# Dilated attention: the queries' and keys' transposes placed between the column blocks of their projection, and the first token tile's merge placed inside the item loop

## The chip, the cores and the metric

The kernel runs on one core of a Trainium2 chip. The metric is the device time of one execution in microseconds; the time before is the median of three executions. TensorE is written PE for its matmuls and PEld for its weight loads, VectorE is DVE, ScalarE is ACT, GpSimd is POOL and SyncE is SP.

## The reference

The program computes two blocks of a transformer-like network one after the other, for 256 tokens of width 1024 in float32. The change is in the last layer of the second block, between two feed-forward parts: attention with three patterns of window and dilation, whose outputs are merged by their log-sum-exp.

```python
ATTN_HEADS = 8
DILATED_PATTERNS = ((128, 1), (512, 4), (2048, 16))
...
def dilated_attention_mixer(u, w_qkv, w_o):
    bsz, seq, _ = u.shape
    qkv = (u @ w_qkv).reshape(bsz, seq, 3, ATTN_GROUPS, ATTN_HEADS, ATTN_HEAD_DIM)
    slopes = jnp.exp2(-8.0 * jnp.arange(1, ATTN_HEADS + 1, dtype=jnp.float32) / ATTN_HEADS)
    outs = []
    lses = []
    for g, (window, dilation) in enumerate(DILATED_PATTERNS):
        o, l = dilated_window_attention(qkv[:, :, 0, g], qkv[:, :, 1, g], qkv[:, :, 2, g], slopes, window, dilation)
        outs.append(o)
        lses.append(l)
    weights = jax.nn.softmax(jnp.stack(lses, axis=0), axis=0)
    merged = jnp.einsum('gblh,gblhd->blhd', weights, jnp.stack(outs, axis=0).astype(jnp.float32))
    return merged.reshape(bsz, seq, ATTN_OUT_WIDTH).astype(u.dtype) @ w_o
```

## The kernel before, in words

**Weights.** All weight matrices stream through one pipeline. A unit is 512 rows by 512 columns, 1 MB. SP loads a unit into one of four `raw` buffers. ACT rounds each half of it to a high part (`whi`, line 321), DVE subtracts to get the low part (`wlo`, line 325), and PE multiplies (lines 377, 378 and 381: high by high, low by high, high by low; 24 matmuls for a unit). ACT and DVE run two units ahead of PE: in its step k (`Split.step`, line 328) ACT splits the first half of unit k+2 once PE has used the first half of unit k, and the second half once PE has used all of unit k. A projection (`project_pe`, `project_act`, `project_dve`, lines 625 to 670) takes two units for a block of 512 output columns; the results of a block collect in a pair of PSUM banks (three pairs in turn: banks 0 to 5), and ACT copies them out at the end of the block (line 654). `s.with_(f)` makes every step call f with the number of the step, after the second half's split.

**The stage.** The projection of queries, keys and values has 4608 columns: 9 blocks, 18 units. Blocks 0 to 2 are the queries of the three patterns, 3 to 5 their keys, 6 to 8 their values. Its output is `p_a`, tokens on the partitions. Queries and keys must be turned, so that the head dimension lies on the partitions: `dil_pe` does it after the last block, in three rounds of 16 transposes (line 2418), all eight PSUM banks in turn. `dil_act` first copies out of a staging area the masks and the slopes (lines 2389 to 2393), and then copies the turned banks into `qTa` and `kTa` (lines 2402 and 2404) and the queries of the odd heads back into `p_a` (line 2405). The third round uses banks of the first, so it waits for ACT's copies out of it. The queries of a block's even head have zeros in partitions 64 to 127, and those of the odd head in 0 to 63; POOL clears the first (line 2385) and DVE the second (line 2735).

**The items.** There are 48 items: for each of two token tiles t, three patterns g, and eight heads. An item (`attn_pe`, `attn_dve`, `attn_act`, lines 1046 to 1129) is: scores by matmul with two added mask terms (PE 1061, 1063), row maximum (DVE 1113), exponential with its row sum (ACT 1128), transposes of the probabilities (PE 1087), their copy (DVE 1104), and their product with the values (PE 1074). The order on each engine is written out by hand: PE does the scores of item i+1, the transposes of item i, then the outputs of item i-1; DVE does the maximum of item i, the copy of item i-1, then whatever `every(i)` adds. Items of tile 0 have 128 keys, those of tile 1 have 256. Every eight items `raw_take` (line 2431) copies the two output banks of a pattern to `y` or `hc`, at i = 9, 17, 25, 33, 41 and after the loop.

**The merge.** After the loop `merge_dve` (lines 2435 to 2459) works out the weights of the patterns for both tiles (five small operations a tile, an exponential on ACT at line 2463, nine small operations a tile) and then scales the three outputs and adds them (five operations of 512 columns a tile). Then come the transposes of the result (`heads_out_pe`, line 1333), the output projection (`out_a`, four units) and the residual.

`Engine.link` puts an instruction and makes the engine wait for its end; `e.after(name)` waits for a named instruction.

## Time and profile before

| | |
|---|---|
| median of 3 executions | 3195.71 us (3195.0 to 3195.91) |
| the profiled execution's own time | 3196.73 us |
| its span | 3194.9 us |
| PE, PEld, DVE, ACT, POOL busy | 2826.9, 2335.9, 1831.3, 1522.7, 147.1 us |
| the projection of this stage, first to last matmul | 2776.4 to 2874.6 us |
| from its last block's copy to the first scores | 2875.7 to 2891.5 us |
| the 48 items | 2891.5 to 2953.4 us |
| the merge, until the first transpose of its result | 2953.4 to 2966.7 us |

Times in rows are microseconds from the start of the span. A row of the timeline gives the start, the time for which the instruction (or the run of equal ones, xN) was busy, engine, line, operation, output<-input with shapes, and in square brackets how long the engine sat idle before it and what it was waiting for. Ends of matmuls are modelled: of a run of matmuls the distance between starts is what one costs.

### The profile page before, as it was taken

Reading aid. Unit: us, or ns where it says so; the run is one execution under the profiler, and the core shown is the slowest. Engines: PE = TensorE matmul, PEld = TensorE weight load, DVE = VectorE, ACT = ScalarE, POOL = GpSimd, SP = SyncE. Lnnn points to the kernel's source line nnn. Section 1 sums busy time; section 2 is a strip of 40 time slices with the busy share of each in tenths; the row PEclk is TensorE's granted clock in tenths of the full one; section 3 lists DMA queues with packets and bytes.
Section 4 is the critical chain, followed back from the end, with each engine's and each line's share of the span. In section 5 each row is a group of like instructions: output and inputs, shape, how many; then the busy total and the mean of one; then the engine's idle time right before and its main releaser. Section 6 shows DMA issues by size and latency. Waiting matters only on the chain.

```text
span 3194.9 us, 34582 instructions
## 1 busy us (share of the span) xinstructions
PE 2826.9 (88%) x13343; PEld 2335.9 (73%) x13343; DVE 1831.3 (57%) x2220; ACT 1522.7 (48%) x2142; POOL 147.1 (5%) x195
## 2 busy tenths in 40 slices
PE   6897689989975877999999899898689989897798
PEld 5775578878864556888888688677578878787587
DVE  5566556656646444555688755447655555545555
ACT  4553245545534323444677644463444444445344
POOL 1012000000011000000000000000100000100000
PEclk8998889999987786999999999899799999999899
DMA  7662146656662003555799845450045545560354
GB/s 254 230 223 72 53 143 226 211 172 220 214 137 92 1 1 125 178 170 170 238 321 330 292 158 182 135 186 12 7 148 166 193 164 177 182 197 17 99 159 143
DMA packets 266417, 511.15 MB, mean 160 GB/s; under 512 B 9252, under 2 KB 40188, under 8 KB 266267
## 3 DMA queue, kind: packets, MB, share of 16 engines
q1 hardware_dynamic: 262320, 498.11, 46.8%
q0 software_dynamic: 3952, 11.07, 1.7%
q8 instruction: 96, 1.57, 0.2%
q14 instruction: 49, 0.40, 0.0%
HBM read 508.05 MB, written 1.05 MB: 159 GB/s over the span
## 4 chain that ended last, share of the span: by engine, by line
PE 80%; DVE 9%; ACT 5%; DMA 3%; issue 2%; POOL 2%; DVEq 0%; ACTq 0%; POOLq 0%; SPq 0%
PE bank L377 22%; PE bank L378 22%; PE bank L381 21%; PE bank L1061 2%; PE bank L1074 2%; DVE wlo L325 2%; PE bank L2030 2%; ACT whi L321 1%; PE bank L1087 1%; PE bank L746 1%; PE bank L1699 1%; DMA raw<-in_od_w_in 1%; PE bank L465 1%; DMA raw<-in_moe_w 1%; PE bank L1736 1%
## 5 line engine op out<-in xcount | busy, mean ns | idle before, releaser
L325 DVE TENSOR_TENSOR wlo<-raw,whi 128x1024 fp32r<-128x1024 f32 (+1 forms) x1012 | 1196.8, 1199 | 910.6 <-ACT whi L321 906.2
L321 ACT ACTIVATE whi<-raw 128x1024 fp32r<-128x1024 f32 (+1 forms) x1012 | 1037.5, 1039 | 902.4 <-PE bank L381 860.5
L377 PE MATMUL bank<-whi,xhi 128*128 128x512 f32 (+2 forms) x2432 | 935.8, 385 | 36.8 <-DVE wlo L325 17.3
L378 PE MATMUL bank<-wlo,xhi 128*128 128x512 f32 (+2 forms) x2432 | 925.8, 381 | 0.0
L381 PE MATMUL bank<-whi,xlo 128*128 128x512 f32 (+2 forms) x2432 | 924.8, 380 | 0.0
L377 PEld LDWEIGHTS bank<-whi,xhi 128*128 128x128 f32 x2432 | 465.5, 191 | 130.2 <-issue 41.3
L381 PEld LDWEIGHTS bank<-whi,xlo 128*128 128x128 f32 x2432 | 464.5, 191 | 83.0
L378 PEld LDWEIGHTS bank<-wlo,xhi 128*128 128x128 f32 x2432 | 465.8, 192 | 79.8
L377 PE MATMUL bank<-whi,f_hhi 128*128 128x512 f32 x528 | 210.3, 398 | 3.1 <-ACT f_gates L781 3.1
L378 PE MATMUL bank<-wlo,f_hhi 128*128 128x512 f32 x528 | 209.3, 396 | 0.0
L381 PE MATMUL bank<-whi,f_hlo 128*128 128x512 f32 x528 | 209.2, 396 | 0.0
L746 PE MATMUL bank<-kb,tmp 128*128 128x128 f32 x224 | 51.7, 424 | 101.4 <-DVE tmp L726 94.9
L1128 ACT ACTIVATE tmp<-bank,negm 128x512 f32<-128x512 f32 (+2 forms) x112 | 60.7, 542 | 141.7 <-DVE negm L1113 110.5
L746 PEld LDWEIGHTS bank<-kb,tmp 128*128 128x128 f32 x224 | 45.5, 226 | 109.8 <-DVE tmp L726 102.3
L377 PEld LDWEIGHTS bank<-whi,f_hhi 128*128 128x128 f32 x528 | 99.6, 189 | 27.5 <-ACT f_gates L781 3.9
L381 PEld LDWEIGHTS bank<-whi,f_hlo 128*128 128x128 f32 x528 | 99.6, 189 | 24.2
L378 PEld LDWEIGHTS bank<-wlo,f_hhi 128*128 128x128 f32 x528 | 99.6, 189 | 23.6
L377 PE MATMUL bank<-whi,m_hhi 128*128 128x512 f32 x242 | 97.1, 401 | 0.2 <-DVE wlo L325 0.2
L378 PE MATMUL bank<-wlo,m_hhi 128*128 128x512 f32 x242 | 95.7, 395 | 0.0
L381 PE MATMUL bank<-whi,m_hlo 128*128 128x512 f32 x242 | 95.7, 395 | 0.0
L1113 DVE TENSOR_REDUCE negm<-bank 128x1 f32<-128x256 f32 (+2 forms) x96 | 46.0, 480 | 74.0 <-PE bank L1063 45.1
L377 PE MATMUL bank<-whi,spad 128*128 128x512 f32 x192 | 79.3, 413 | 9.4 <-DVE wlo L325 9.2
(449 smaller groups left out, 2692.0 us busy)
## 6 DMA issues: line engine op xcount, KB each, us to landing
raw<-in_ffn_w SPq DMA_DIRECT2D x180, 1024.0 KB, 5.1
raw<-in_moe_w SPq DMA_DIRECT2D x96, 1024.0 KB, 6.0
raw<-in_ada_w SPq DMA_DIRECT2D x48, 1024.0 KB, 5.9
raw<-in_moe_w SPq DMA_DIRECT2D x48, 768.0 KB, 4.6
raw<-in_ev_w_in SPq DMA_DIRECT2D x24, 1024.0 KB, 6.1
raw<-in_ffn_w SPq DMA_DIRECT2D x36, 512.0 KB, 3.6
raw<-in_hyb_w_in SPq DMA_DIRECT2D x18, 1024.0 KB, 5.0
raw<-in_attn_w_qkv SPq DMA_DIRECT2D x18, 1024.0 KB, 5.1
```

Of the source, the lines that this page charges most:

```text
L321: nc.scalar.activation(whole, part, ACT.Copy).then_inc(sem("w_hi"), 1)
L325: nc.vector.tensor_tensor(wlo[s][:, 0:rows, 0:n], part, whole.bitcast(F32), ALU.subtract)\
L377: nc.tensor.matmul(bank[:, 0:n], xk_h, whi[s][:, wk, 0:n], start=first, stop=False)
L378: ins = nc.tensor.matmul(bank[:, 0:n], xk_h, wlo[s][:, wk, 0:n], start=False, stop=last and xl is None)
L381: ins = nc.tensor.matmul(bank[:, 0:n], xk_l, whi[s][:, wk, 0:n], start=False, stop=last)
L465: ins = nc.tensor.transpose(T[f // 2][:, c:c + P], hs[:, t, f * P:f * P + P], ident)
L746: ins = nc.tensor.transpose(banks[b][:, c:c + P], tmp[:, t, kk * P:kk * P + P], ident)
L1061: nc_last = nc.tensor.matmul(bank[:, 0:n], it["q"], it["k"], start=True, stop=not adds)
L1074: ins = nc.tensor.matmul(it["o"], probT[i % 2][:, k * P:k * P + P], it["v"][k], start=k == 0, stop=k == kt - 1)
L1113: nc.vector.tensor_reduce(col, SC[i % 2][:, 0:it["n"]], AX.X, ALU.max, negate=True)\
L1128: nc.scalar.activation(prob[i % 2][:, 0:it["n"]], SC[i % 2][:, 0:it["n"]], ACT.Exp, bias=negm[:, i:i + 1], accum_out=den[:, i:i + 1]).then ...
L2030: ins = nc.tensor.matmul(to, diagonal_tap(k, j), hpad[:, k, j:j + TOK], start=j == 0, stop=j == TAPS - 1)
```

## The change

1. `dil_pe` becomes a step of the projection: after blocks 1 to 6, PE turns the block before, eight transposes into banks 6 and 7 (which the projection doesn't use), after ACT's copies of the round before. It first waits until all blocks but the last one computed are copied out.
2. `dil_act` becomes a step of the weight pipeline on ACT: masks and slopes after units 1, 3 and 5; the turned blocks after units 4, 6, ..., 14, four copies for a block of queries and two for one of keys.
3. The odd heads' queries go to `gates[:, 1, :]`, `hc[:, 1, :]` and the first 1024 columns of `p_a`. POOL clears all the zero parts; DVE's clearing is gone. POOL's last one waits for the third round of transposes, and the loading of a gain row into `gates[:, 0, :]` is queued behind it.
4. Tile 0 is merged in the item loop: DVE's steps are attached to items 27 to 36, and ACT's exponential to item 30. Its result goes to `y` instead of `tmp`.

```diff
+    odd_rows = [gates[:, 1, :], hc[:, 1, :], p_a[:, 0, 0:D]]
...
-        return p_a[:, b // 6, b % 6 * TOK:b % 6 * TOK + TOK] if odd else qTa[:, b, :]
+        return odd_rows[b // 4][:, b % 4 * TOK:b % 4 * TOK + TOK] if odd else qTa[:, b, :]
...
+        e.after("rb0:h")
+        for rows_ in odd_rows[0:2]:
+            e.link(nc.gpsimd.memset(rows_[0:HD, :], 0.0))
         e.link(nc.gpsimd.memset(qTa[HD:P, :, :], 0.0), "qa zeros")
...
+        e.after("dilT2")
+        e.link(nc.gpsimd.memset(odd_rows[2][0:HD, :], 0.0), "qa last zeros")
+
+    def dil_act(e, i):
+
+        if i == 1:
+            loaded(e, "dil0", 2)
+            e.put(nc.scalar.activation(flat3(dist[:, :, :]), stage_d[:, 0:N], ACT.Copy))
+            e.put(nc.scalar.activation(one[:, :], ident, ACT.Copy))
+        if i == 3:
+            e.put(nc.scalar.activation(dil[:, :, :, :].rearrange("p g t k -> p (g t k)"), stage_d[:, N:4 * N], ACT.Copy))
+        if i == 5:
+            for hd in range(8):
+                e.put(nc.scalar.activation(slope[:, hd, :], ident, ACT.Copy, scale=2.0 ** -(hd + 1)), "masks")
+        if i % 2 == 0 and 4 <= i < 4 + 2 * 6:
+            r = i // 2 - 2
             e.after(f"dilT{r}")
             if r == 0:
-                e.after("dilT1")
+                e.after("qa zeros")
+            for b in range(2):
+                at = 4 * (r % 3) + 2 * b
+                if r >= 3:
+                    e.put(nc.scalar.activation(flat3(kTa[:, at:at + 2, :]), T[b][:, :], ACT.Copy), f"dilqk{r}")
+                    continue
+                e.put(nc.scalar.activation(flat3(qTa[0:HD, at:at + 2, :]), T[b][0:HD, :], ACT.Copy, scale=HD ** -0.5))
+                e.put(nc.scalar.activation(odd_rows[r][HD:P, 2 * b * TOK:2 * b * TOK + 2 * TOK], T[b][HD:P, :], ACT.Copy,
+                                           scale=HD ** -0.5), f"dilqk{r}")
+
+    def dil_pe(e, i):
+
+        if 1 <= i <= 6:
+            r = i - 1
+            e.eng.wait_ge(sem("out_done"), e.outs.n - 1)
+            if r:
+                e.after(f"dilqk{r - 1}")
             for b in range(4):
...
+                for t in range(NT):
+                    c, at = (b % 2) * TOK + t * P, r * N + b * P
+                    ins = nc.tensor.transpose(T[b // 2][:, c:c + P], p_a[:, t, at:at + P], ident)
             e.put(ins, f"dilT{r}")
...
     def dil_every(e, base):
         def every(i):
             if i >= 9 and (i - 9) % 8 == 0:
                 raw_take((i - 9) // 8)
+            for at, part in ((27, merge_low_dve), (30, merge_share_dve)):
+                if i == at:
+                    part(e, base, 0)
+            if i in (31, 32, 34):
+                merge_scale_dve(e, 0, (31, 32, 34).index(i))
+            if i in (35, 36):
+                merge_add_dve(e, 0, i - 34, raw_out(0))
...
     def merge_dve(e, base):
...
+        merge_low_dve(e, base, 1)
+        merge_share_dve(e, base, 1)
+        for g in range(3):
+            merge_scale_dve(e, 1, g)
+            if g:
+                merge_add_dve(e, 1, g, tmp[:, 1, 0:N])
+
+    def merge_act(e, t):
+        e.after(f"merge low{t}")
+        e.link(nc.scalar.activation(negm[:, 24 * t:24 * t + 24], negm[:, 24 * t:24 * t + 24], ACT.Exp),
+               f"weight exps{t}")
...
-                resid2_pool(e, "rb1", 5, 1, 5, "rb0:h", 0.5)
+                resid2_pool(e, "rb1", 5, 1, 5, "rat:h", 0.5)
...
+                s.with_(lambda i: dil_act(e, i))
                 project_act(e, s, D, QKV, lambda t, c, n: p_a[:, t, c:c + n])
-                dil_act(e)
-                attn_act(e, ATT0[4], A_ITEMS)
-                merge_act(e)
+                s.with_(None)
+                attn_act(e, ATT0[4], A_ITEMS, lambda i: merge_act(e, 0) if i == 30 else None)
+                merge_act(e, 1)
...
-                e.after("dilT1")
-                e.link(nc.vector.memset(p_a[0:HD, :, 0:1536], 0.0), "qa odd zeros")
...
-                project_pe(e, s, [(xhi, xlo, KD)], QKV, "in_at")
-                dil_pe(e)
+                project_pe(e, s, [(xhi, xlo, KD)], QKV, "in_at", lambda i: dil_pe(e, i))
+                e.eng.wait_ge(sem("out_done"), e.outs.n)
                 attn_pe(e, ATT0[4], A_ITEMS, lambda e, i: e.after(f"raw{i // 8 - 2}") if i % 8 == 0 and i >= 16
-                        else None, "dilqk2", "masks", "qa zeros", "qa odd zeros")
-                heads_out_pe(e, "att_a")
+                        else None, "dilqk2", "dilqk5", "masks", "qa last zeros")
+                heads_out_pe(e, "att_a", lambda t: tmp[:, 1, :] if t else raw_out(0))
```

`merge_low_dve(e, base, t)` has the five small operations of a tile, `merge_share_dve` the nine others, `merge_scale_dve` one scaling and `merge_add_dve` one addition of 512 columns: the operations of lines 2442 to 2459, tile by tile.

## Rows read from the trace of the kernel before

**Rows 1.** The page: its first line, the span.
```profile
span 3194.9 us, 34582 instructions
```

**Rows 2.** Two stretches: length, busy (count) of PE, PEld, DVE, ACT, POOL, clock, DMA.
```profile
2776.40:2874.60 98.20, 98.20 (x432) 81.04 (x432) 46.53 (x41) 45.73 (x54) 7.15 (x5) 1.00 0.60 193
2875.70:2892.20 16.50, 7.81 (x52) 7.35 (x52) 3.84 (x2) 15.21 (x31) 0.00 (x0) 0.88 0.22 72
```

**Rows 3.** The timeline from the last block's copy to the first probabilities' transposes.
```profile
2875.61 1.06 ACT L321 ACTIVATE whi<-raw 128x1024 fp32r<-128x1024 f32 x1
2875.77 3.72 PE L2418 MATMUL bank<-kb,a_p 128*128 128x128 f32 x32 [1.18 <-ACT a_p L654]
...
2876.70 1.23 DVE L325 TENSOR_TENSOR wlo<-raw,whi 128x1024 fp32r<-128x1024 f32 x1 [2.40 <-ACT whi L321]
...
2885.24 3.40 PE L2418 MATMUL bank<-kb,a_p 128*128 128x128 f32 x16 [5.74 <-ACT a_p L2405]
...
2887.71 3.74 ACT L2402 ACTIVATE a_kT<-bank 128x512 f32<-128x512 f32 x6
...
2891.50 0.70 PE L1061 MATMUL bank<-a_kT,a_qT 128*128 128x128 f32 x2 [2.87 <-ACT a_kT L2402]
...
2892.64 0.29 DVE L1113 TENSOR_REDUCE negm<-bank 128x1 f32<-128x128 f32 x1 [9.82 <-PE bank L1063]
...
2893.01 1.28 ACT L1128 ACT_TABLE_LOAD   x1 [1.56 <-DVE negm L1113]
...
2894.81 0.48 PE L1087 MATMUL bank<-kb,tmp 128*128 128x128 f32 x1 [1.43 <-ACT tmp L1128]
```

**Rows 4.** PE's timeline in a feed-forward part: eight transposes in a stream of matmuls.
```profile
3025.05 1.04 PE L465 MATMUL bank<-kb,tmp 128*128 128x128 f32 x8
...
3026.16 0.40 PE L378 MATMUL bank<-wlo,xhi 128*128 128x512 f32 x1
```

**Rows 5.** The timeline in the items of tile 1: exponentials 33, 36 and 41, and DVE.
```profile
2930.95 0.47 ACT L1128 ACTIVATE tmp<-bank,negm 128x256 f32<-128x256 f32 x1 [0.77 <-DVE negm L1113]
...
2931.16 0.88 DVE L2431 COPY y<-bank 128x256 f32<-128x256 f32 x2
...
2935.20 0.47 ACT L1128 ACTIVATE tmp<-bank,negm 128x256 f32<-128x256 f32 x1 [1.01 <-DVE negm L1113]
...
2938.75 0.42 DVE L1113 TENSOR_REDUCE negm<-bank 128x1 f32<-128x256 f32 x1 [0.58 <-PE bank L1063]
...
2941.88 0.47 ACT L1128 ACTIVATE tmp<-bank,negm 128x256 f32<-128x256 f32 x1 [0.77 <-DVE negm L1113]
```

**Rows 6.** The timeline of the merge, tile 0 and tile 1, and what follows it.
```profile
2953.39 0.17 DVE L2442 TENSOR_TENSOR ss<-negm 128x8 f32<-128x8 f32 x1
...
2954.39 0.17 DVE L2442 TENSOR_TENSOR ss<-negm 128x8 f32<-128x8 f32 x1
...
2955.74 0.57 DVE L2450 TENSOR_TENSOR den<-den,negm 128x8 f32<-128x8 f32 x3 [0.38 <-ACT negm L2463]
...
2961.21 0.57 DVE L2450 TENSOR_TENSOR den<-den,negm 128x8 f32<-128x8 f32 x3
...
2966.70 1.97 PE L1333 MATMUL bank<-kb,tmp 128*128 128x128 f32 x8 [14.27 <-DVE tmp L2459]
```

**Rows 7.** ACT's timeline: exponentials 4 and 6 of the items.
```profile
2899.09 0.37 ACT L1128 ACTIVATE tmp<-bank,negm 128x128 f32<-128x128 f32 x1 [0.83 <-DVE negm L1113]
...
2900.92 0.37 ACT L1128 ACTIVATE tmp<-bank,negm 128x128 f32<-128x128 f32 x1 [0.61 <-DVE negm L1113]
```

**Rows 8.** Stretches of one microsecond in which the granted clock changed, columns as in rows 2.
```profile
2884.00:2885.00 1.00, 0.00 (x0) 0.00 (x0) 0.00 (x0) 0.97 (x2) 0.00 (x0) 0.90 0.00 0
2891.00:2892.00 1.00, 0.50 (x3) 0.50 (x3) 0.00 (x0) 0.45 (x1) 0.00 (x0) 0.82 0.00 0
2898.00:2899.00 1.00, 1.00 (x9) 1.00 (x9) 0.24 (x3) 0.26 (x2) 0.00 (x0) 0.77 0.00 0
...
2976.00:2977.00 1.00, 1.00 (x4) 0.78 (x3) 0.00 (x0) 0.65 (x1) 0.00 (x0) 0.52 0.00 0
```

More of the change, by code:

```diff
@@ L2461, in merge_act, with merge_low_dve @@
-    def merge_act(e):
-        e.after("weights")
-        e.link(nc.scalar.activation(negm[:, 0:48], negm[:, 0:48], ACT.Exp), "weight exps")
+    grp = lambda ap, t, g: ap[:, (t * 3 + g) * 8:(t * 3 + g) * 8 + 8]
+    def merge_low_dve(e, base, t):
+        e.eng.wait_ge(sem("exp_done"), base + 24 * (t + 1))
+        e.eng.wait_ge(sem("max_done"), base + 24 * (t + 1))
+        low = ss[:, t * 8:t * 8 + 8]
+        e.link(nc.vector.tensor_tensor(low, grp(negm, t, 0), grp(negm, t, 1), ALU.min))
+        e.link(nc.vector.tensor_tensor(low, low, grp(negm, t, 2), ALU.min))
+        for g in range(3):
+            e.link(nc.vector.tensor_tensor(grp(negm, t, g), low, grp(negm, t, g), ALU.subtract), f"merge low{t}")
@@ new lines, in merge_share_dve @@
+    def merge_share_dve(e, base, t):
+        e.after(f"weight exps{t}")
+        z = ss[:, t * 8:t * 8 + 8]
+        for g in range(3):
+            e.link(nc.vector.tensor_tensor(grp(den, t, g), grp(den, t, g), grp(negm, t, g), ALU.mult))
+        e.link(nc.vector.tensor_tensor(z, grp(den, t, 0), grp(den, t, 1), ALU.add))
+        e.link(nc.vector.tensor_tensor(z, z, grp(den, t, 2), ALU.add))
+        e.link(nc.vector.reciprocal(z, z))
+        for g in range(3):
+            e.link(nc.vector.tensor_tensor(grp(negm, t, g), grp(negm, t, g), z, ALU.mult))
@@ new lines, in merge_scale_dve, with merge_add_dve @@
+    def merge_scale_dve(e, t, g):
+        part = raw_out(t * 3 + g)
+        e.link(nc.vector.tensor_tensor(heads(part), heads(part), over(grp(negm, t, g), 8, HD), ALU.mult))
+    def merge_add_dve(e, t, g, to):
+        former = raw_out(t * 3) if g == 1 else to
+        e.link(nc.vector.tensor_tensor(to, former, raw_out(t * 3 + g), ALU.add), "att_a:o")
+    def merge_dve(e, base):
+        merge_low_dve(e, base, 1)
+        merge_share_dve(e, base, 1)
+        for g in range(3):
+            merge_scale_dve(e, 1, g)
+            if g:
+                merge_add_dve(e, 1, g, tmp[:, 1, 0:N])
```

60 lines of the change are left out of this document (5 added, 55 removed).

## The prediction

> **What bounds the kernel now.** I read the busy times by stretch first [rows 2]. In the projection PE is busy for all of its 98.2 us at full clock, while ACT is busy for 45.7 and DVE for 46.5: a unit takes 98.2 / 18 = 5.46 us of PE, and ACT and DVE have room. In the 16.5 us behind it this turns round: ACT is busy for 15.2 us, PE for 7.8. Then I read the timeline of that stretch [rows 3]. PE starts the first 32 transposes at 2875.77, waits 5.7 us for ACT's copies, turns the last 16, waits 2.9 us again, and starts the scores at 2891.50. So 15.7 us lie between the end of the projection and the items, and ACT sets them. The third view is the merge [rows 6]: from 2953.39 to 2966.70 DVE works alone, and PE sits idle for 14.3 us. The fourth is the item loop [rows 5]: there PE has no idle time in an ordinary item, and DVE has 0.58 us of it in each. The change works at the two ends where PE waits, and pays for it inside two stretches where PE is the bound.
>
> **Part 1, queries and keys.** The moment to compare is the first transpose of probabilities, 2894.81 before [rows 3].
>
> What is added to PE's projection: the same 48 transposes, in six groups of eight. The trace has such a group in a stream of weight matmuls [rows 4]: the group starts at 3025.05, and the second matmul behind it at 3026.16. These 1.11 us hold one matmul of the stream, whose pitch is 98.2 / 432 = 0.23 us [rows 2], so a group costs 0.88 us and six cost 5.3 us. Bounds: by the pitch of the 32 transposes in a row, 3.72 / 32 = 0.116 us [rows 3], 48 cost 5.6 us; nothing below 4.5 us is plausible, as the array must do the work, and at half clock (3.40 / 16 = 0.21 us, same rows) it would be 10.2 us, but the projection runs at full clock. I take 5.3, since that row has the same surroundings.
>
> What is added to ACT there: what it does in the 16.5 us less the split of a weight half (1.06 us [rows 3]), 14.2 us. Its 45.7 us become 60 in a projection of 103.5 us. The worst step is one with four copies of queries. ACT does half a split at the end of a unit (1.06 us) and then four copies of 3.74 / 6 = 0.62 us [rows 3], and is done 3.6 us after the end of the unit. Three are waiting for it: its own next split, which would have started half a unit, 2.7 us, after that end, and is 0.9 us late where it leads PE by two units, some 10.9 us; DVE's subtraction and with it SP's release of a `raw` buffer, late by the same 0.9 us; and PE, whose next group needs the copies at the end of the next unit, 5.46 us after, so 1.8 us of slack. The copies of output blocks come behind ACT's step by as much, and PE needs a pair of banks only two blocks later. So all of it costs nothing while this slack holds. POOL's clearings are short beside the projection; the gain row queued behind the last one is needed only for the residual after the output projection, over 100 us later. PE's added wait for the blocks copied out asks for the block before the last one, a whole block (10.9 us) old. DVE loses a clearing that nobody would wait for now.
>
> What remains behind the projection: before, ACT copied the last block out and split half of a unit (2875.61, 1.06 us), and DVE subtracted it from 2876.70 to 2877.93 [rows 3], in the shadow of the transposes. That shadow is gone. PE can do the first scores as soon as the last block is copied out, at 2875.77 plus the 5.3, but DVE's first maximum now stands behind that subtraction. From the start of the first maximum to the first transpose of probabilities it took 2894.81 - 2892.64 = 2.17 us before, the 1.28 us of a table load on ACT among them [rows 3]; the table load waits for that maximum in both kernels. So the new moment is 2877.93 + 0.02 + 2.17 + 5.3 = 2885.4, and the gain is 2894.81 - 2885.4 = **9.4 us**. If DVE's subtraction did not stand in the way it would be 1.2 us more; if the groups cost 7 us, it would be 1.7 us less.
>
> **Part 2, the merge.** Saved behind the loop is tile 0's share [rows 6]: its first five operations, 2954.39 - 2953.39 = 1.00 us, and the others, 2961.21 - 2955.74 = 5.47 us, together 6.5 us. The rest stays: tile 1's part, the exponential, the transposes.
>
> Paid in the loop: the same 6.5 us of DVE, in items 27 to 36. The trace shows what an insertion of that kind costs. `raw_take` puts 0.91 us of DVE work behind item 33 (0.88 and the gap to the next instruction); exponentials 33 to 36 are 4.25 us apart, while five ordinary items take 2941.88 - 2935.20 = 6.68 us, 1.34 each, so three take 4.01 and the cost is 0.24 us [rows 5]. An insertion X thus costs X - 0.67 where it stands alone. In a row of such items DVE has only its 0.58 us an item to give. So: the five small operations at item 27, 1.00 us, cost 0.3; the nine at item 30 (eight like 2953.39's at 0.20 us and a reciprocal at 0.23) are 1.83 us and cost 1.2; five insertions of 512 columns, (5.47 - 1.83) / 5 = 0.73 us each [rows 6], cost 0.73 - 0.58 = 0.15 each, 0.75; item 33's `raw_take` has no reserve from ordinary neighbours any more, 0.1. The sum is 2.3 us. ACT's exponential at item 30 lies in its 0.77 us of waiting for the maximum [rows 5]. Bounds: nothing, if PE's queue takes it up; all 6.5 us, if nothing is hidden. I take 2.3, as `raw_take` is the same kind of work in the same place. The gain of part 2 is 6.5 - 2.3 = **4.2 us**.
>
> **The clock.** At the start of the items the clock was at half (1.2 GHz): it fell in 2884 to 2885 after five idle microseconds of PE, fell again in 2891 to 2892 after PE's next wait and rose in 2898 to 2899 [rows 8]. The first exponential came at 2893.01 + 1.28 = 2894.29 [rows 3], the fifth at 2899.09; by the later pace, 1.83 us for two [rows 7], these four items would have taken 3.7 us instead of 4.8, so the half clock cost 1.1 us. After the change PE still idles 1.2 us before the first scores and some 3 us between them and the first transposes of probabilities, with about one microsecond of work between. I take the same cost again. Behind the merge the clock rose only in 2976 to 2977 [rows 8], about six microseconds into the output projection; PE's idle time there shrinks from 14.3 to 7.8 us, which is still longer than the five after which it fell in rows 8, so this cost stays too. Either place may come out up to 1.5 us better or 1 us worse.
>
> The Trainium skill (TensorE: Matmul & The Clock Gate, HAM oscillation) says that idle gaps between bursts of matmuls throttle PE, and that the phase in which the chip looks is not tied to the kernel. By it the two places are drawn anew by any shift of the work, which is what the last sentence allows for. No run here shows it yet.
>
> **Sum.** 9.4 + 4.2 = 13.6 us. The profiled span of 3194.9 us [rows 1] becomes 3181.3; the profiled execution's own time, 3196.73, becomes 3183.1; the median of the runs shown, 3195.71, which lies 0.8 us above the span, becomes **3182.1**.
>
> **Rivals.**
>
> *The merge's gain is given back in the loop.* An item is a ring: maximum, exponential, transposes, copy. If DVE's added operations delay a maximum and PE has nothing queued, each insertion costs its full time. For it: an ordinary item leaves DVE 0.58 us of idle time, and yet an insertion of 0.91 us already stretches the loop, so PE's queue holds little in reserve. Against: `raw_take` costs 0.24 of 0.91 us [rows 5]. Then part 2 gives 0 and the time is 3195.7 - 9.4 = 3186.3. Chance 0.15.
>
> *The clock stays at full at the start of the items.* PE's longest idle stretch there would be some 3 us, while the fall in 2884 to 2885 came after more than five [rows 3, 8]. Against: the second fall, in 2891 to 2892, came after 2.9 us. It would give 1.1 us more: 3181.0. Chance 0.12.
>
> *Transposes in the projection cost what one of them lasts.* By two rows, 32 of them lasting 3.72 us and eight lasting 1.04 us [rows 3, 4], the pitch is 2.68 / 24 = 0.11 us and a single one lasts 1.04 - 7 x 0.11 = 0.26 us. If each drained before the next, 48 would cost 12.5 us instead of 5.3; the gain falls to 13.6 - 7.2 = 6.4 us and the time is 3189.3, at the edge of 0.2%. Against: eight lasted 1.04 us in all, in a stream [rows 4]. Chance 0.04. The Trainium skill (TensorE: Matmul & The Clock Gate, Part 4) gives about 275 ns for a transpose in one kernel's context and says that transposes don't bring the clock up; by it the sum would be that of this rival. The trace doesn't agree on either: the pitch is 0.116 us [rows 3].
>
> *Slower: ACT's copies late by a unit.* If PE reached groups 2 to 6 before ACT had copied the round before, each would wait; the transposes stand between two blocks in PE's order, so the whole stream waits with them. It decides from a lag of 1.8 us on, and takes away the 13.6 us when the five waits are 2.7 us each. With ACT late by one whole unit, each wait is 5.46 - 1.8 = 3.7 us, 18.5 in all: 3195.7 - 13.6 + 18.5 = 3200.6. For it: PE already waited 5.7 and 2.9 us for just these copies [rows 3]. Against: ACT is busy for only 60 of 103.5 us, and its steps are tied to PE's own units. Chance 0.04.
>
> **How the numbers follow.** The forecast, with both gains to within their bounds, has 0.62; the rivals have 0.15, 0.12, 0.04 and 0.04; 0.03 is left for what I don't see. A measurement of this kernel can tell about 0.2%, 6.4 us, from no change. Faster by more than that are the forecast and the first two rivals (0.89, and half of the rest: 0.91); within it is the rival of the long transposes (0.05); slower is the last (0.04). The range runs from both clocks better and a cheaper loop (3182.1 - 3 = 3179, rounded) to the first rival with 1 us more for the groups, 3187.3.
>
> **What would show it.** In the changed profile: the projection longer by 5.3 us, with PE's idle time in it at zero (right) or with waits of PE for line 2402's or 2404's successors (the last rival); first scores about 1.2 us after the last matmul, and DVE's first maximum directly behind a `wlo` subtraction; the exponentials of items 30 to 37 some 1.5 us apart, with one interval near 2.5 us; about 6.8 us from DVE's first merge operation behind the loop to the transposes; granted clock at half for 3 to 7 us in the first items. The prediction is wrong if PE waits in the projection, if items 27 to 37 stretch by more than 4 us together, or if something outside the stage moves by more than the clock can.

## The result, and the profile after

| | before | after |
|---|---|---|
| median of 7 executions each, on one chip, us | 3195.91 (3192.74 to 3199.8) | 3180.21 (3174.9 to 3187.13) |
| ratio of the two, 95% interval | | 0.9949 (0.9936 to 0.9962) |
| profiled execution: own time, span | 3196.73, 3194.9 | 3180.21, 3178.3 |

The change takes 0.5% off, 15.7 us by the medians and 16.6 by the spans. The forecast was 13.6 us. The page of the changed kernel:

```profile
span 3178.3 us, 34595 instructions
```

To see where the time went I cut the stage at moments that both traces have: ACT's copies of the first and of the last block of the projection, the first transposes of probabilities, the exponentials of items 0, 24 and 47, the first transpose of the result, and ACT's first copy of sums in the output projection. All in us, each a difference of two starts in the timelines:

| stretch | before | after | difference | forecast |
|---|---|---|---|---|
| first to last block's copy | 87.04 | 92.52 | +5.48 | +5.3 |
| last copy to first transposes of probabilities | 20.17 | 4.04 | -16.13 | -14.7 |
| exponential 0 to 24 | 24.50 | 24.30 | -0.20 | 0 |
| exponential 24 to 47 | 31.35 | 32.99 | +1.64 | +2.3 |
| exponential 47 to the result's first transpose | 16.55 | 10.06 | -6.49 | -6.5 |
| that transpose to the first sums | 12.73 | 11.72 | -1.01 | 0 |
| first copy to first sums, whole | 191.83 | 175.12 | -16.71 | -13.6 |

(Exponential 0 lies 0.51 us ahead of its transposes in both traces, so the differences add up, though the stretches overlap by that.) Outside the two ends almost nothing moved: the first copy stands at 2787.60 before and 2787.66 after, and from the first sums to the end it is 215.5 us in both.

The front, PE, ACT and DVE after the last block, the rows that answer to [rows 3]:

```profile
2880.18 1.08 ACT L654 ACTIVATE a_p<-bank 128x512 f32<-128x512 f32 x2 [1.60 <-PE bank L381]
2881.15 1.06 ACT L321 ACTIVATE whi<-raw 128x1024 fp32r<-128x1024 f32 x1
2881.32 0.49 PE L1061 MATMUL bank<-a_kT,a_qT 128*128 128x128 f32 x2 [1.17 <-ACT a_p L654]
2882.23 1.28 ACT L1129 ACT_TABLE_LOAD   x1
2882.25 1.23 DVE L325 TENSOR_TENSOR wlo<-raw,whi 128x1024 fp32r<-128x1024 f32 x1 [2.41 <-ACT whi L321]
2883.39 0.48 DVE L1113 TENSOR_REDUCE negm<-bank 128x1 f32<-128x128 f32 x2
2883.71 0.37 ACT L1129 ACTIVATE tmp<-bank,negm 128x128 f32<-128x128 f32 x1 [0.19 <-DVE negm L1113]
2884.22 0.48 PE L1087 MATMUL bank<-kb,tmp 128*128 128x128 f32 x1 [1.79 <-ACT tmp L1129]
```

PE waits 1.17 us for the last copy and 1.79 us for the first exponential, where it waited 1.18, 5.74, 2.87 and 1.43 us before. The row to look at is the table load: it starts at 2882.23, right behind ACT's last split, while DVE is still subtracting. In [rows 3] the load came at 2893.01, behind the first maximum. Here only the maximum is left between the subtraction and the exponential.

A group of transposes in the projection, PE's timeline, to be read as [rows 4]:

```profile
2798.12 0.39 PE L381 MATMUL bank<-whi,xlo 128*128 128x512 f32 x1
2798.35 1.03 PE L2430 MATMUL bank<-kb,a_p 128*128 128x128 f32 x8
...
2799.45 0.39 PE L378 MATMUL bank<-wlo,xhi 128*128 128x512 f32 x1
```

The stretch of the projection, columns as in [rows 2]:

```profile
2778.00:2881.00 103.00, 102.14 (x474) 84.67 (x472) 42.90 (x35) 59.11 (x82) 10.00 (x8) 1.00 0.56 187
```

PE is busy for 102.1 of 103.0 us; the rest is the 1.17 us wait at its end. ACT has 59.1 us, for which the forecast said 60. How close it comes to PE shows where ACT has four copies of queries and PE comes back for the banks. There are three such places; these are ACT's rows in the first, and then PE's next group:

```profile
2807.70 0.59 ACT L2417 ACTIVATE gates<-bank 64x512 f32<-64x512 f32 x1
...
2810.34 1.09 ACT L654 ACTIVATE a_p<-bank 128x512 f32<-128x512 f32 x2 [0.96 <-PE bank L381]
...
2810.15 1.03 PE L2430 MATMUL bank<-kb,a_p 128*128 128x128 f32 x8
```

The last copy ends at 2807.70 + 0.59 = 2808.29, PE needs it at 2810.15: 1.86 us of slack, for which the forecast said 1.8 (the other two places have 1.85 and 1.83).

In the loop, DVE's timeline from the last of the nine small operations on, and then ACT's exponentials around them:

```profile
2917.81 0.57 DVE L2474 TENSOR_TENSOR negm<-negm,ss 128x8 f32<-128x8 f32 x3
2918.41 0.42 DVE L1113 TENSOR_REDUCE negm<-bank 128x1 f32<-128x256 f32 x1
2918.75 0.41 DVE L1104 COPY tmp<-bank 128x256 f32<-128x256 f32 x1
2919.08 0.68 DVE L2478 TENSOR_TENSOR y<-y,negm 128x512 f32<-128x512 f32 x1
2919.80 0.42 DVE L1113 TENSOR_REDUCE negm<-bank 128x1 f32<-128x256 f32 x1
```

```profile
2916.41 0.47 ACT L1129 ACTIVATE tmp<-bank,negm 128x256 f32<-128x256 f32 x1 [0.93 <-ACT negm L2494]
...
2918.87 0.47 ACT L1129 ACTIVATE tmp<-bank,negm 128x256 f32<-128x256 f32 x1 [1.89 <-DVE negm L1113]
...
2920.25 0.47 ACT L1129 ACTIVATE tmp<-bank,negm 128x256 f32<-128x256 f32 x1 [0.82 <-DVE negm L1113]
...
2921.64 0.47 ACT L1129 ACTIVATE tmp<-bank,negm 128x256 f32<-128x256 f32 x1 [0.82 <-DVE negm L1113]
```

The nine small operations end at 2918.38, and only then comes the maximum; the exponential behind it is 2.46 us after the one before it, where an ordinary item takes 1.34. DVE runs without a gap from there on, and the items with an operation of 512 columns are 1.38 us apart.

Behind the loop, DVE's first merge operation, the first after the exponential, and the result's transposes, as in [rows 6]:

```profile
2944.24 0.17 DVE L2460 TENSOR_TENSOR ss<-negm 128x8 f32<-128x8 f32 x1
...
2945.56 0.57 DVE L2469 TENSOR_TENSOR den<-den,negm 128x8 f32<-128x8 f32 x3 [0.36 <-ACT negm L2494]
...
2951.06 0.48 PE L1334 MATMUL bank<-kb,y 128*128 128x128 f32 x1 [7.78 <-DVE tmp L2482]
```

From 2944.24 to 2951.06 it is 6.8 us, as forecast, and PE's idle time there is 7.8 instead of 14.3 us. The clock, one microsecond each, as in [rows 8]:

```profile
2884.00:2885.00 1.00, 0.78 (x4) 0.78 (x5) 0.27 (x1) 0.52 (x4) 0.00 (x0) 0.52 0.52 55
2887.00:2888.00 1.00, 1.00 (x9) 1.00 (x8) 0.43 (x3) 0.46 (x2) 0.00 (x0) 0.77 0.95 369
2945.00:2946.00 1.00, 0.00 (x0) 0.00 (x0) 0.54 (x5) 0.22 (x1) 0.00 (x0) 0.74 0.00 0
2959.00:2960.00 1.00, 1.00 (x5) 0.76 (x5) 0.00 (x0) 0.00 (x0) 0.00 (x0) 0.93 0.00 0
```

It is at half from 2884.0 until 2887.5, and again from 2945.5 until 2959.1.

### The profile page after: what moved, and what is told of

It is laid out like the page before. It is cut to its first block, busy times and chain, and to the rows that moved or that the text cites. A ratio compares the mean times of both kernels' runs of the same rounds, so it can differ in the third digit from the quotient of the medians.

```text
span 3178.3 us, 34595 instructions
## 1 busy us (share of the span) xinstructions
PE 2823.1 (89%) x13343; PEld 2332.3 (73%) x13343; DVE 1826.7 (57%) x2219; ACT 1522.6 (48%) x2143; POOL 150.2 (5%) x198
## 4 chain that ended last, share of the span: by engine, by line
PE 82%; DVE 9%; ACT 4%; DMA 2%; issue 2%; POOL 2%; DVEq 0%; ACTq 0%; POOLq 0%; SPq 0%
PE bank L377 23%; PE bank L378 22%; PE bank L381 22%; PE bank L1061 2%; PE bank L1074 2%; PE bank L2031 2%; DVE wlo L325 2%; PE bank L1087 1%; ACT whi L321 1%; DMA raw<-in_od_w_in 1%; PE bank L746 1%; PE bank L1700 1%; PE bank L465 1%; PE bank L1737 1%; POOL ss L687 1%
## 5 line engine op out<-in xcount | busy, mean ns | idle before, releaser
L551 DVE TENSOR_TENSOR f_hlo<-bank,f_hhi 128x512 fp32r<-128x512 f32 (+1 forms) x66 | 42.8, 686 | 78.0 <-ACT f_hhi L513 78.0
```

Source lines behind the costliest of these rows:

```text
L551: ins = nc.vector.tensor_tensor(hlo[:, at, :].rearrange(flat), T[b // TOK][:, 0:k * TOK], hhi[:, at, :].bitcast(F32).rearrange(flat), ALU. ...
```

## The experiments

Every kernel computes the whole of the program; none leaves work out. e4 repeats copies with the same values, and e7 to e9 add transposes that nobody reads. e3 to e7 were executed once each (3201.07, 3200.23, 3192.70, 3177.53 and 3182.02 us); as the program's time scatters by more than most of these edits are worth, they are read from their stretches.

**Do the parts add up?** e1 is the changed kernel with both tiles merged behind the loop again; e2 is the kernel before with the merge of tile 0 moved into the loop.

```diff
e1:             raw_take((i - 9) // 8)
-            for at, part in ((27, merge_low_dve), (30, merge_share_dve)):
...
     def merge_dve(e, base):
+        merge_low_dve(e, base, 0)
         merge_low_dve(e, base, 1)
```

```diff
e2:             raw_take((i - 9) // 8)
+            for at, part in ((27, merge_low_dve), (30, merge_share_dve)):
...
-                heads_out_pe(e, "att_a")
+                heads_out_pe(e, "att_a", lambda t: tmp[:, 1, :] if t else raw_out(0))
```

> Part 1 alone: queries and keys turned inside the projection, the whole merge behind the loop as before. If the two parts are independent, the first transposes of probabilities come 4.0 us after the start of the last block's copy (before: 20.2), the six groups cost 0.91 us each, the loop from exponential 24 to 47 takes 31.35 us as before, and the merge to the first transpose of its result 16.55 us as before. Net 16.1 - 5.5 = 10.7 us: a median near 3185. Rival (the parts lean on each other: the loop's insertions cost more or less where the loop starts earlier): the loop or the merge differ from before by more than 0.3 us. The clock at the two restarts may move the median by 1.5 us either way.

> Part 2 alone: the turning behind the projection as before, tile 0 merged in the loop. Independent parts: 20.2 us from the last block's copy to the first transposes of probabilities as before, the loop from exponential 24 to 47 at 33.0 us (1.6 more than before), and 10.1 us from exponential 47 to the first transpose of the result (6.5 less). Net 4.85 us: a median near 3191, 1.5 us either way for the clock. Rival: ACT's exponential at item 30 or the loop behaves differently without part 1; then the loop is not at 33.0.

| | first to last copy | to transposes of prob. | exp 0 to 24 | 24 to 47 | 47 to result's transposes | first copy to first sums | median (runs) | ratio |
|---|---|---|---|---|---|---|---|---|
| e1 | 92.53 | 4.04 | 24.23 | 31.37 | 16.55 | 179.64 | 3184.37 (10) | 0.9964 (0.9952 to 0.9977) |
| e2 | 87.03 | 20.32 | 25.32 | 32.97 | 10.08 | 187.75 | 3196.36 (10) | 0.9996 (0.9983 to 1.0010) |

Each part alone changes its own stretches by what the changed kernel shows, to within 0.2 us, and leaves the others alone, but for 0.8 us in e2's first 24 items, where the clock was at half until 2904.3, 6.6 us into the items instead of 4.2. Part 1 is worth 191.83 - 179.64 = 12.2 us of the stage, part 2 4.1 us; together they make 16.3 of the 16.7. Yet e2's program isn't faster: its span is 3194.8 us with a stage that is 4 us shorter. e11 is e2 again in more executions, and e10 the changed kernel beside it:

> Part 2 alone once more. In its stage it saved 4.85 us by the profile of e2, but the whole program's median did not move (interval of the ratio 0.9983 to 1.001). Theory: the gain is there and the program's own scatter of several us hides it; with more runs the ratio comes out near 0.9985, and the stage's stretches repeat to 0.1 us. Rival (something behind or ahead of the stage takes it back): the ratio stays at 1.000 with an interval that excludes 0.9985, and the time from the first sums to the end is longer than the 215.5 us of the other kernels.

> The changed kernel itself, on the same chip as e9 and e11, for the whole program's time: its profiles so far put the stage 16.6 us below the kernel before, of which 1 to 2 us are clock. A ratio near 0.9950, and lower by 6 us than e11. In its profile the stretches of the stage (copy of the first block to the last 92.5 us, 4.04 us to the first transposes of probabilities, 33.0 us for exponentials 24 to 47, 10.06 us from there to the result's transposes) should come back to 0.1 us, while everything ahead of the stage may lie up to 8 us elsewhere.

Part 2 again: stage 186.13 us (-5.7), median 3192.67 (12 runs, 3184.88 to 3198.8), ratio 0.9989 (0.9976 to 1.0002). The changed kernel again: stage 175.42 us (-16.4), median 3182.41 (7 runs), ratio 0.9961 (0.9947 to 0.9975); the kernel before beside both 3196.13 (18 runs, 3188.27 to 3209.35). So the whole program scatters by some 10 to 20 us, and the stage does not: e2's and e11's stages differ by 1.6 us, nearly all of it in the two stretches where the clock is at half. The 13 profiles tell where it comes from: the first copy of this stage stands anywhere between 2782.2 and 2797.2 us, whereas from the first sums to the end it is 215.4 to 215.5 us in eleven of them. The other two are e2 and e11, both with 216.2: there the stretch from the issue of the last DMA to the end of the span is 5.2 us instead of 4.4. So the rival of e11's expectation is half right: part 2 alone loses 0.8 us at the very end of the program, outside its stage and not in the changed kernel. Why is open. Part 2's gain of 4 to 6 us is shown in the stage (against the one profile of the kernel before); in the time of the program it isn't resolved by 22 runs.

**Why did the table load come early?** Two things might have moved it: that ACT's last work before the items is now a split and no longer `dil_act`'s copies, or how those copies are put. `link` makes ACT wait for its own copy's end. e3 is the kernel before with `put` in the place of `link` for the three copies, so that the later instructions don't wait for ACT itself.

```diff
-                    e.link(nc.scalar.activation(flat3(kTa[:, at:at + 2, :]), bank[:, :], ACT.Copy), f"dilqk{r}")
+                    e.put(nc.scalar.activation(flat3(kTa[:, at:at + 2, :]), bank[:, :], ACT.Copy), f"dilqk{r}")
```

> The kernel before, with ACT not waiting for each of its own copies of the turned blocks (the copies are independent). Theory: in the kernel before the table load stood behind the first maximum because ACT's last instruction before the items was followed by a wait for itself; without that wait the table load of 1.28 us starts as soon as the last copy is issued, near 2891.4, and is over before the first maximum is there. The first transposes of probabilities come 1.1 to 1.4 us earlier after the last block's copy (18.8 to 19.0 instead of 20.2). Rival (the table load always waits for what its exponential waits for, and in the changed kernel something else hid it): 20.2, less 0.5 at most for the copies' own waits.

ACT's load, DVE's first maximum and the first exponential in e3:

```profile
2898.22 1.28 ACT L1128 ACT_TABLE_LOAD   x1
...
2899.48 0.29 DVE L1113 TENSOR_REDUCE negm<-bank 128x1 f32<-128x128 f32 x1 [9.44 <-PE bank L1063]
...
2899.80 0.37 ACT L1128 ACTIVATE tmp<-bank,negm 128x128 f32<-128x128 f32 x1 [0.30 <-DVE negm L1113]
```

The load starts 1.26 us before the maximum and no longer 0.37 us behind it as in [rows 3]; the exponential comes 0.32 us after the maximum's start. From the first scores to the first transposes of probabilities it is 2.06 instead of 3.31 us, and the scores come 0.47 us sooner after the last block's copy. So the load can run ahead of the wait for the maximum, and in the kernel before it did not because of ACT's waits for itself. That wait was long over: the last copy ended at 2891.45 and the load came at 2893.01. The records of ACT's sequencer show what it did. In the kernel before two waits stand in front of the first exponential; the one for the maximum is an instruction of its own, at 2892.96, and the load comes behind it, while the exponential carries the wait for ACT itself. In e3 and in the changed kernel there is one wait, the exponential carries it, and the load comes ahead. e2 and e11, which kept `link`, have the separate wait and the late load; e1 has neither. Part 1 takes that away in passing. It is a gain of 1.25 us that needs no transposes in the projection.

**Does the front hang on ACT's slack of 1.8 us?** e4 makes ACT's copies in the projection three times as many, each awaited, so that they end after PE has come back.

```diff
-            for b in range(2):
+            for b in (0, 1) * 3:
...
-                    e.put(nc.scalar.activation(flat3(kTa[:, at:at + 2, :]), T[b][:, :], ACT.Copy), f"dilqk{r}")
+                    e.link(nc.scalar.activation(flat3(kTa[:, at:at + 2, :]), T[b][:, :], ACT.Copy), f"dilqk{r}")
```

> The changed kernel with ACT's copies of every turned block made three times (the same values again). A block of queries then takes 12 x 0.62 = 7.4 us instead of 2.5 behind the half split of 1.0, so it is done 8.4 us after its unit's end, where PE asks 5.46 us after. If the slack is what the prediction worked out (1.8 us, one wait for each of the groups 2, 3 and 4), PE waits 2.9 us before each of these three groups and not before those behind keys (4.7 us after the end): the projection is longer by 8.8 us. Rival (the weight pipeline's lead of two units takes it up): PE waits less than 1 us in all. Other rival (ACT, with 12.7 us of work for a block of 11.8, starves the weight matmuls): waits of line 377 for wlo.

The projection is 107.32 us, 14.8 more than after; 8.8 were expected. PE's waits in it (what waited, what for; us, times, longest), and the clock behind the first:

```profile
PE bank L2430 <- ACT a_p L2417: 3.2, 1, 3.2
...
PE bank L2430 <- ACT hc L2417: 3.1, 1, 3.1
PE bank L2430 <- ACT gates L2417: 3.1, 1, 3.1
```

```profile
2816.00:2817.00 1.00, 0.28 (x2) 0.31 (x3) 0.00 (x0) 0.97 (x2) 0.00 (x0) 0.73 0.00 0
2817.00:2818.00 1.00, 1.00 (x6) 1.00 (x5) 0.31 (x1) 0.98 (x2) 0.00 (x0) 0.50 0.00 0
...
2819.00:2820.00 1.00, 1.00 (x4) 0.81 (x3) 0.25 (x1) 1.00 (x3) 0.00 (x0) 0.56 0.08 16
```

The waits stand where the theory put them and sum to 9.4 us. The other 5.4 us are the clock: at each wait the clock fell to half for 3.4 us (2816.5 to 2819.9, 2833.5 to 2837, 2850.6 to 2854), which costs 1.8 us a time. A wait of 3.1 us costs 4.9. The rival of ACT's late copies is real, then, and its price was put too low in the prediction; in the changed kernel it doesn't come into play.

**What do insertions in the loop cost?** e5 puts all five operations of 512 columns behind item 35; e6 spreads the small ones over items 26, 27, 29, 30 and 31 (two, three, three, three, three), with ACT's exponential at item 29 instead of 30, and has the large ones behind 32, 34, 35, 36 and 37.

```diff
e5:
-            if i in (31, 32, 34):
-                merge_scale_dve(e, 0, (31, 32, 34).index(i))
-            if i in (35, 36):
-                merge_add_dve(e, 0, i - 34, raw_out(0))
+            if i == 35:
+                for g in range(3):
+                    merge_scale_dve(e, 0, g)
+                for g in (1, 2):
+                    merge_add_dve(e, 0, g, raw_out(0))
e6:
-            for at, part in ((27, merge_low_dve), (30, merge_share_dve)):
-                if i == at:
-                    part(e, base, 0)
-            if i in (31, 32, 34):
+            if 26 <= i <= 31:
+                merge_small_dve(e, base, i)
+            if i in (32, 34, 35):
```

> The changed kernel with tile 0's three scalings and two additions all behind item 35, instead of behind 31, 32, 34, 35 and 36. Theory: DVE has 0.67 us an item to give, counted from start to start (an item takes 1.34 us of the loop and 0.67 us between the starts of DVE's two instructions and the next one), and gives it anew in each item. Five insertions of 0.72 us then cost 0.05 each when spread, and 5 x 0.72 - 0.67 = 2.9 us in one item: exponentials 24 to 47 take 35.6 us or so instead of 33.0. Rival (PE's queue takes up what DVE is late, wherever it is put): 33.0 as before. With 0.58 us an item, as predicted, the spread ones would have cost 0.15 each and the bunch 3.0: the bunch alone doesn't tell these two apart, the spacing of 1.38 to 1.39 us in the changed kernel does.

> The changed kernel with tile 0's fourteen small operations spread over items 26, 27, 29, 30 and 31 (0.4 to 0.6 us each, under the 0.67 us that an item gives), and the large ones behind 32, 34, 35, 36 and 37. In the changed kernel the nine at item 30 cost 1.1 us and the five at item 27 0.26. Theory: both costs go; exponentials 24 to 47 take 31.35 + 5 x 0.05 = 31.6 to 31.9 us instead of 33.0, and nothing else changes. Rival (DVE's waits for its own small results, not their sum, stretch an item): 32.5 or more.

e5: 35.58 us from exponential 24 to 47. Two exponentials in a row of ACT, the second behind the insertion:

```profile
2933.70 0.47 ACT L1129 ACTIVATE tmp<-bank,negm 128x256 f32<-128x256 f32 x1 [0.53 <-DVE negm L1113]
...
2938.12 0.47 ACT L1129 ACTIVATE tmp<-bank,negm 128x256 f32<-128x256 f32 x1 [3.85 <-DVE negm L1113]
```

They are 4.42 us apart for 3.6 us of DVE. This item takes 1.58 us in the kernel before, so it costs 2.84 us, where the theory of 0.67 us of room says 2.9. e6: 31.80 us, 0.45 above the 31.35 of a loop that has no merge in it, while 10.24 us follow the loop instead of 10.06. (From the first copy to the first sums e6 has 174.95 us, only 0.2 less than the changed kernel: its output projection, from the result's first transpose to the first sums, took 12.59 us instead of 11.72, at a clock that came back later.) The same 6.5 us of DVE cost 4.2 us in one form, 1.64 in the changed kernel and 0.45 spread out. An item gives DVE room once, and only for what is inserted in that item.

**What does the half clock cost?** e7 keeps PE busy over its two gaps: 14 transposes of the identity behind the scores of item 1, and 62 before the transposes of the result.

```diff
+            if i == 0 and len(items) == 48:
+                for _ in range(14):
+                    nc.tensor.transpose(psum[7][:, 0:P], ident, ident)
...
+                for _ in range(62):
+                    nc.tensor.transpose(psum[0][:, 0:P], ident, ident)
```

> The changed kernel with transposes of the identity on PE that nobody reads: 14 behind the first two scores, 62 while DVE merges tile 1 behind the loop. Theory: PE's half clock at both restarts comes from its idle time, and transposes count as activity. Then the granted clock stays at 1.0 from the end of the loop on; the eight transposes of the result take 0.9 us to the next instruction instead of 1.7, and the first 9 or so matmuls of the output projection run at 0.23 us instead of 0.43: from exponential 47 to the first sums of squares 19.0 to 19.3 us instead of 21.8. At the start of the items the clock stays at 1.0, and exponentials 0 to 24 take 23.2 us instead of 24.3. Rival (transposes do not count as activity): the clock falls as before and both stretches are unchanged, or longer by what the fill runs over.

The items' first 24 in e7 and in the changed kernel, then the merge's transposes and what follows in e7:

```profile
2888.50:2911.00 22.50, 20.71 (x164) 18.80 (x165) 13.98 (x51) 10.22 (x46) 0.00 (x0) 1.00 0.16 48
```

```profile
2884.20:2908.00 23.80, 21.54 (x165) 20.07 (x165) 13.87 (x51) 10.28 (x46) 0.00 (x0) 0.93 0.14 45
```

```profile
2946.20 6.93 PE L2861 MATMUL bank<-kb 128*128 128x128 f32 x62
...
2954.14 0.33 PE L1337 MATMUL bank<-kb,y 128*128 128x128 f32 x1 [1.01 <-DVE tmp L2485]
...
2957.32 0.67 PE L377 MATMUL bank<-whi,xhi 128*128 128x512 f32 x1 [2.09 <-DVE xlo L1031]
```

```profile
2957.00:2958.00 1.00, 0.68 (x2) 0.61 (x3) 0.97 (x3) 0.00 (x0) 0.00 (x0) 0.71 0.00 0
```

At the front the theory holds: clock 1.00 throughout, and 23.13 us between exponentials 0 and 24 instead of 24.30, 1.17 us less; the prediction had put 1.1 us on that half clock. At the merge it holds by half: the result's transposes start at full clock and are 0.11 us apart instead of 0.21. But then PE waits 2.1 us for the first operand of the output projection, the clock falls at 2957.4 and rises at 2960.8, and from exponential 47 to the first sums it is 20.58 us (21.78 after) where 19.0 to 19.3 were expected.

**Is there a version that beats both?** e8 takes e6 and e7 together, with the two things that still stand before the first exponential out of the way: a tiny exponential on ACT in the projection's step 15 makes it load the table there, and DVE's last subtraction is held until items 38 and 39, half in each. e9 drops the 14 transposes at the start, has 68 in the place of the 62, and puts 16 more between the result's transposes and the output projection.

```diff
+        if i == 15:
+            e.put(nc.scalar.activation(cmp2[:, 0:2], ident[:, 0:2], ACT.Exp))
...
+                def every(i):
+                    every_(i)
+                    if i in (38, 39):
+                        s.held(i - 38)
...
e9 only:
+                for _ in range(16):
+                    nc.tensor.transpose(psum[0][:, 0:P], ident, ident)
                 follow(e, s, "cat_a", 2)
```

> The changed kernel with the small operations spread, the transposes that keep the clock, an exponential of two columns put on ACT in the projection's unit 15 (so that the table load lies there), and DVE's last subtraction of the projection moved behind items 38 and 39 in two halves, so that the first maximum doesn't wait for it. Expected beside the changed kernel, in the stage: 1.1 to 1.4 us from the last block's copy to the first transposes of probabilities (2.7 us instead of 4.0), 1.1 us in items 0 to 24, 1.2 us in items 24 to 47, 2.6 us from there to the first sums: 6 us in all, a median near 3174. Rival (the loop pays for the moved subtraction): the items from 24 to 47 take more than 32.0 us.

> As e8, with the fill of transposes where it was found to be missing or in the way: none behind the first scores (there it delayed the first transposes of probabilities by 1.1 us, and with DVE's subtraction moved away PE hardly idles), 68 instead of 62 behind the loop, and 16 more behind the transposes of the merged result, where PE idled for 2.1 us and the clock still fell. Expected beside e8: the first transposes of probabilities 2.5 us after the last block's copy instead of 3.6; no half clock at the start of the items; no half clock in the output projection, so 6.6 us instead of 7.35 from its first matmul to the first sums. From the first block's copy to the first sums 169.3 us or so, where the changed kernel has 175.1 and the one before 191.8. Rival (PE's first idle stretches still bring the clock down): half clock for 3 us in the first items, 0.5 to 1 us lost again.

In e8 3.64 us lie between the last copy and the transposes of probabilities instead of 2.7: the 14 filling transposes stood in the way of the turning of the first exponential, which began at 2878.57 and takes 0.37 us.

```profile
2878.50 1.72 PE L1103 MATMUL bank<-kb 128*128 128x128 f32 x14
...
2878.57 0.37 ACT L1151 ACTIVATE tmp<-bank,negm 128x128 f32<-128x128 f32 x1
...
2880.05 0.27 PE L1109 MATMUL bank<-kb,tmp 128*128 128x128 f32 x1
```

In e9, without that filling, the gaps have become so short that the clock stayed up (in the one profile there is):

```profile
2878.18 0.49 PE L1080 MATMUL bank<-a_kT,a_qT 128*128 128x128 f32 x2 [1.18 <-ACT a_p L673]
...
2879.71 0.33 PE L1106 MATMUL bank<-kb,tmp 128*128 128x128 f32 x1 [0.43 <-ACT tmp L1148]
```

```profile
2879.70:2902.30 22.60, 20.75 (x165) 18.88 (x165) 14.12 (x51) 10.36 (x46) 0.00 (x0) 1.00 0.00 1
2934.20:2953.60 19.40, 17.82 (x130) 16.02 (x129) 10.81 (x29) 3.08 (x7) 0.00 (x0) 1.00 0.00 1
```

| | last copy to transposes of prob. | exp 0 to 24 | 24 to 47 | 47 to result's transposes | first copy to first sums | median (runs) | ratio |
|---|---|---|---|---|---|---|---|
| after, e10 | 4.03 | 24.24 | 32.98 | 10.06 | 175.42 | 3182.41 (7) | 0.9961 (0.9947 to 0.9975) |
| e8 | 3.64 | 24.03 | 31.79 | 10.42 | 171.45 | 3175.95 (6) | 0.9935 (0.9923 to 0.9947) |
| e9 | 2.67 | 23.14 | 31.84 | 10.42 | 169.02 | 3174.59 (6) | 0.9937 (0.9923 to 0.9952) |

(In e8 exponential 0 lies 1.48 us ahead of its transposes and not 0.51, so its 24.03 us hold the delay by the filling; its clock was at 1.00.) From its first matmul of the output projection to the first sums e9 takes 5.8 us, where 6.6 were expected.

e9's stage is 6.4 us shorter than that of the changed kernel run on the same chip beside it, and its median 7.8 us lower; the executions lie between 3170.58 and 3179.38 us against 3179.12 and 3187.97. Its stage is the shortest of this study, 22.8 us below that of the kernel before. e8 and e9 can't be told apart by the program's time.

## Why the prediction was right, and where its steps were off

The time, 3180.2 us, lies 1.9 us below the forecast of 3182.1 and inside its range. Step by step:

- **Transposes in the projection, 5.3 us.** Measured 5.48. The same two rows as in [rows 4] give 2799.45 - 2798.12 less the pitch of two matmuls, 2 x 0.23, so 0.87 us for a group here; over the whole stretch it is 5.48 / 6 = 0.91. The rival of 0.26 us for each transpose is refuted. Of transposes and the clock the prediction also says that the trace disagrees, but its row shows the pitch alone. The kernel before has rows for it: from 2885.24 on the 16 transposes of the third round are all that PE does, and the clock rises among them, near 2888.2.

```profile
2887.00:2888.00 1.00, 1.00 (x6) 1.00 (x6) 0.00 (x0) 0.94 (x3) 0.00 (x0) 0.50 0.00 0
2888.00:2889.00 1.00, 0.63 (x5) 0.40 (x3) 0.00 (x0) 0.94 (x3) 0.00 (x0) 0.89 0.00 0
```

- **ACT's copies cost nothing while 1.8 us of slack hold.** The slack was 1.86 us, and PE had no wait. e4 shows that this was the condition: with the copies late, the waits came.
- **The first transposes of probabilities, 9.4 us earlier, net.** It was 16.13 - 5.48 = 10.65. The step that failed is "the table load waits for that maximum in both kernels". It did not: it ran beside DVE's subtraction, and 1.2 us were won. e3 shows the reason, ACT's waits for its own copies in the kernel before, which put the wait for the maximum ahead of the load. The 2.17 us from the maximum to the transposes were carried over as one piece; they held a part whose place was set by something that the change removes.
- **The loop, 2.3 us.** It was 1.64. Item 27's small operations cost 0.26 (forecast 0.3), item 30's 1.11 (1.2); the term that was mis-sized is that of the large ones: about 0.05 each and not 0.15, and nothing for item 33's `raw_take`, for which 0.1 was added. I had set the room of an item at DVE's idle time, 0.58 us. The right figure was the 0.67 that `raw_take` had given, X - 0.67: 0.73 - 0.67 = 0.06. DVE's instructions overlap a little, the next one starting 0.34 us after one that lasts 0.42 (2918.41 and 2918.75 above), so idle time counted from an end to a start is less than the room.
- **The merge behind the loop, 6.5 us.** It was 6.49. e1 and e2 show that it belongs to part 2 alone.
- **The clock, no change.** In the items it held: 24.30 against 24.50 us. In the output projection it did not: the clock came back at 2959.1, 4 us after the first matmul there instead of 6.2, and 1.0 us was won. The prediction had allowed up to 1.5 us for it. Why the clock comes back sooner isn't settled; e1, with PE's idle time of before, has the short stretch too (7.38 us from the first matmul to the first sums, after 7.66, before 8.66). And e2, with the shorter idle time, has a long one (8.49). So it isn't the shorter gap. e3 has the same merge, gap and output projection as the kernel before, and 7.44 us where that has 8.66. The Trainium skill says (TensorE: Matmul & The Clock Gate, What's actually happening in Part 1; the prediction named another section, HAM oscillation) that the chip's watch on PE runs freely and is not tied to the kernel's start. The traces fit this: over all runs with a merge that PE sits out, this stretch was between 7.4 and 8.7 us, whatever the edit. This 1.0 us is luck, then, and no gain of the change.

Taken together, 1.2 us at the front, 0.7 in the loop, 0.2 in the first items and 1.0 in the output projection are the 3.1 us by which the stage did better than forecast (16.7 against 13.6). The first two belong to the change, the last two go with the clock.

The rivals: the loop gives back 1.64 of 6.49 us, so the first falls; the second asked for full clock at the start of the items, and it was at half until 2887.5, for 3.5 us; the third and the fourth fall with the first two points.

## What to carry to other kernels

Work of an engine is cheapest in a stretch where another engine is the bound: ACT's copies cost nothing in the projection, while PE's own transposes there cost their full 5.5 us. What has to be worked out is the slack until the bound comes back for the result, here 1.8 us for each group, and not the share of busy time. What is inserted in a loop of items costs what exceeds the room of its own item, so it is spread in pieces below that room (0.67 us here) and never put in one place. Before carrying a stretch over as one piece, ask of each instruction in it which wait holds it there. Where an exponential that needs a table load follows a wait of ACT for itself, that wait is worth removing.

## What the runs showed of the hardware

- A wait of PE of 3.1 us in a stream of matmuls went with a fall of the clock to half for 3.4 us each time, three times out of three, and so cost 1.8 us more than itself (e4). Waits of 1.0 and 2.1 us with 0.9 us of transposes between them went with a fall too (e7; in e8 it fell at 2949.4, after waits of 1.4 and 2.1 us).
- Transposes alone brought the clock from half to full near 2888.2 (kernel before), and transposes of the identity alone kept it at 1.00 over a merge in which PE had nothing else to do: 62 of them in 6.93 us in e7, and with 16 more in the second gap the clock stayed at 1.00 until the first sums of the output projection (e9, one profile). Transposes are 0.11 us apart at full clock and 0.21 at half.
- ACT's table load of 1.28 us runs ahead of the wait for the exponential's operand where the exponential has that one wait; where a wait of ACT for its own earlier instruction is added, the operand's wait becomes an instruction of its own and the load comes behind it (e3 against the kernel before); and an exponential on two columns, placed where ACT had room, took it off the path altogether (e8, e9).
- The times of the program scatter by 10 us and more while the stretches of this stage repeat to within some 0.2 us, clock aside. In the 13 profiles the scatter arises ahead of the stage, where the first copy moves over 15 us, so an edit worth 4 us is read from the trace, and not from the time.
